# An S5 state loop on one core: VectorE works a tile off inside its bank, and output products go two tiles at a time

## The reference

```python
u = h @ w_in
bu_re, bu_im = (einsum('sbgk,gpk->sbgp', u, bb) for bb in (bb_re, bb_im))
_, _, xr, xi = lax.associative_scan(combine, (a_re, a_im, bu_re, bu_im), axis=0)
y = einsum('sbgp,gkp->bsgk', xr, c_re) - einsum('sbgp,gkp->bsgk', xi, c_im)
y = gelu(y + d_skip * u)
y = y * sigmoid(y @ w_glu)
return y @ w_o
```

## Time and profile before

| | |
|---|---|
| Time, median of 3 runs | 2179.3 us (2178.06 to 2179.93) |
| The profiled execution | 2181.11 us, of which the span from first to last instruction 2179.3 us |
| TensorE, VectorE, ScalarE, GpSimd busy | 94%, 32%, 18%, 5% of the span |
| Mean granted clock of TensorE | 0.974 of full speed |
| First product of the state loop on VectorE | 1126.11 us after the span's start |
| Last GLU block | starts at 1292.72 us |

### The profile page before, as it was taken

One profiled execution on the slowest core, in us unless ns is written; L12 is line 12 of the kernel. 1 busy time (PEld: TensorE's weight loads), 2 busy tenths in 40 slices (PEclk: granted clock), 3 DMA queues, 4 the chain that ended last, 5 costly groups with the idle time before them and its releaser, 6 DMA issues.

```text
span 2179.3 us, 29172 instructions
## 1 busy us (share of the span) xinstructions
PE 2054.0 (94%) x12304; PEld 1142.9 (52%) x12304; DVE 688.5 (32%) x1417; ACT 388.9 (18%) x821; POOL 110.9 (5%) x103
## 2 busy tenths in 40 slices
PE   7998999998999999999989985999999999999995
PEld 5577785666785766777755543233323233333322
DVE  3263212344201475344459864101101010101103
ACT  3212103212101322243320002110101010110100
POOL 0000000000000000000027640000000000000000
PEclk9999999999999999999999997999999999999998
DMA  7244465333456322433222114597988989797981
GB/s 300 82 187 156 193 241 224 116 140 143 181 232 244 135 79 87 165 151 139 116 97 107 48 75 166 232 394 299 386 329 343 377 336 383 316 404 298 391 327 58
DMA packets 41488, 472.75 MB, mean 217 GB/s; under 512 B 4645, under 2 KB 6309, under 8 KB 7881
## 3 DMA queue, kind: packets, MB, share of 16 engines
q1 hardware_dynamic: 38576, 464.39, 53.5%
q10 hardware_dynamic: 2568, 6.31, 0.8%
q0 software_dynamic: 272, 1.05, 0.1%
HBM read 470.68 MB, written 1.06 MB: 216 GB/s over the span
## 4 chain that ended last, share of the span: by engine, by line
PE 86%; DVE 7%; DMA 4%; ACT 1%; issue 1%; POOL 0%; ACTq 0%; SPq 0%; DVEq 0%; POOLq 0%
PE bank L896 19%; PE bank L545 14%; PE bank L926 10%; PE bank L848 7%; PE bank L860 3%; PE bank L712 3%; PE bank L530 3%; PE bank L537 3%; PE bank L718 3%; PE bank L558 2%; DMA arena<-in_wgu 2%; PE bank L976 2%; PE bank L967 2%; PE bank L1019 1%; PE bank L615 1%; PE bank L647 1%
## 5 line engine op out<-in xcount | busy, mean ns | idle before, releaser
L896 PE MATMUL bank<-arena 128*32 128x512 f32 x4096 | 451.8, 593 | 1.7 <-DMA arena<-in_wgu 1.4
L545 PE MATMUL bank<-arena 128*128 128x256 f32 x1408 | 321.3, 388 | 11.0 <-ACT small L1236 11.0
L545 PEld LDWEIGHTS bank<-arena 128*128 128x128 f32 x1408 | 270.7, 194 | 67.4 <-issue 17.8
L896 PEld LDWEIGHTS bank<-arena 128*32 128x32 f32 x4096 | 130.0, 110 | 309.7 <-issue 295.8
L926 PE MATMUL bank<-arena 128*32 128x512 f32 x2112 | 238.2, 595 | 0.0
L1996 DVE TENSOR_TENSOR arena<-arena,bank 128x256 f32<-128x256 f32 x64 | 26.9, 421 | 620.7 <-ACT arena L1400 584.3
L848 PE MATMUL bank<-arena 128*128 128x256 f32 x704 | 153.7, 379 | 0.1
L848 PEld LDWEIGHTS bank<-arena 128*128 128x128 f32 x704 | 133.6, 190 | 21.8 <-issue 4.1
L926 PEld LDWEIGHTS bank<-arena 128*32 128x32 f32 x2112 | 62.9, 109 | 133.3 <-issue 132.5
L1400 ACT ACTIVATE arena<-bank 128x256 f32<-128x256 f32 x64 | 24.5, 383 | 580.8 <-PE bank L896 580.8
L2206 POOL TENSOR_TENSOR arena<-arena 128x512 f32<-128x512 f32 x64 | 81.3, 1271 | 45.1 <-DVE arena L2045 42.6
(11 more groups left out here) (422 smaller groups left out, 2024.5 us busy)
## 6 DMA issues: line engine op xcount, KB each, us to landing
arena<-in_wgu SPq DMA_DIRECT2D x88, 2048.0 KB, 9.3
arena<-in_w SPq DMA_DIRECT2D x46, 2048.0 KB, 7.9
arena<-in_wdn SPq DMA_DIRECT2D x88, 1024.0 KB, 7.9
arena<-in_modw SPq DMA_DIRECT2D x24, 2048.0 KB, 9.1
arena<-in_wf SPq DMA_DIRECT2D x11, 3072.0 KB, 10.2
arena<-in_flt_deltas ACTq DMA_DIRECT2D x2, 1024.0 KB, 14.2
cst<-in_consts SPq DMA_DIRECT2D x1, 1162.0 KB, 16.7
arena<-in_x SPq DMA_DIRECT2D x1, 1024.0 KB, 5.2
```

The costliest lines, as they stand in the source:

```text
L545: ins = mm(bank[b][:, j * S:(j + 1) * S], w[:, col:col + P], hT[:, k, :], start=(k == 0), stop=(k == KT - 1))
L896: ins = mm(bank[w % 2][32 * j:32 * j + 32, :], hTe[:, k, TOK * b:TOK * b + TOK], wslot[c % RING][:, k, :], start=(k == 0), stop=(k == KT - ...
```

## The change

- VectorE (loop at L2025): the product with the cosine still goes to SBUF (`vcos`), that with the sine goes in place over the bank. The sum (formerly GpSimd's) and the difference are written into the bank too, each with one operand from `vcos` and one from the bank. The scans read the bank and come in the same step as the products. TensorE may fill the bank again after the scans (`z5_ready`), no longer after the products.
- GpSimd (L2199) keeps the two products into `cz`, which has four buffers instead of two.
- TensorE (L1029): `s5_out(o)`, in even steps, does the output products of tiles `o` and `o + 1` together, in step `o + 4`, alternating between the two tiles, which write different groups of 32 rows of the bank.
- `s5_in` blocks come a step earlier (odd steps); the GLU blocks stay. `y_tile(j)` comes in step `4j + 8` of VectorE, after the scans of tile `4j + 8` (it was after those of tile `4j + 6`).
- `w3[4]` lands at another place and is issued at `cz_ready` 12 instead of 8.

```diff
--- before.py
+++ after.py
@@ -20,7 +20,7 @@
 STATE_TILES = 32
 FR = 3
 FUSES = [len(range(r, 11, FR)) if r < FR else 0 for r in range(RING)]
-IN_HALF = {2: (1, 0), 4: (1, 1), 6: (2, 0), 8: (2, 1), 10: (3, 0), 12: (3, 1)}
+IN_HALF = {1: (1, 0), 3: (1, 1), 5: (2, 0), 7: (2, 1), 9: (3, 0), 11: (3, 1)}
 GLU_AT = {15: 0, 17: 1, 19: 2, 21: 3, 25: 4, 29: 5, 33: 6}
 TWO_PI = 6.283185307179586
 PI2_HI = 6.28125
@@ -315,8 +315,8 @@
 
         uT = view(CH * 2, 8, S)
         yT = view(CH * 2 + 2048, 8, S)
-        vpr = view(CH * 3, 2, 2, 2, S)
-        cz = view(CH * 3 + 2048, 2, 2, 2, S)
+        vcos = view(CH * 3, 2, 2, S)
+        cz = [view(at, 2, 2, S) for at in (CH * 3 + 2048, CH * 3 + 3072, W + 18432, LOW + 2048)]
         sgl = view(CH * 3, 8, S)
         zz = view(W + 2048, 2, 2, S)
         ftmp5 = view(W + 2560, 512)
@@ -332,7 +332,7 @@
         bst = [view(W + 16384, 1024), view(W + 18432, 1024)]
         cst5 = view(W, 2, 1024)
         cneg = view(W + 16384, 1024)
-        wmix = [ring[0], ring[1], ring[0], ring[1], view(LOW + 2048, CH), view(W + 5376, CH)]
+        wmix = [ring[0], ring[1], ring[0], ring[1], view(LOW + 4096, CH), view(W + 5376, CH)]
 
 
 
@@ -409,7 +409,7 @@
                 elif n < 4:
                     sp.wait_ge(sm["grp_ps"], G3 + 4)
                 else:
-                    sp.wait_ge(sm["cz_ready"], (8, 20)[n - 4])
+                    sp.wait_ge(sm["cz_ready"], (12, 20)[n - 4])
                 sp.dma_start(wmix[n], a["w3"][n]).then_inc(landeds[n % RING], 16)
                 if n == 1:
 
@@ -1026,6 +1026,23 @@
             gate_rows(3, gdiag5)
             s5_in(0, 1)
             pe.wait_ge(sm["b5t_ready"], 4)
+            def s5_out(o):
+
+                j = o // 4
+                if o == 0:
+                    pe.wait_ge(sm["c5_ready"], 1)
+                    pe.wait_ge(sm["gb_ready"], 3)
+                pe.wait_ge(sm["cz_ready"], o + 2)
+                if o % 4 == 0 and o >= 8:
+                    pe.wait_ge(sm["y_out"], j - 1)
+                for n, (which, tb, ri) in enumerate(((cst5[:, 0], 0, 0), (cneg, 1, 1), (cst5[:, 1], 0, 1), (cst5[:, 1], 1, 0))):
+                    for q in (o, o + 1):
+                        r = slice(32 * (q % 4), 32 * (q % 4) + 32)
+                        ins = mm(bank[6 + j % 2][r, 0:S], which[:, q * 32:(q + 1) * 32], cz[q % 4][:, tb, ri, :],
+                                 start=(n == 0), stop=(n == 3), skip_group_check=True)
+                        if n == 3:
+                            ins.then_inc(sm["sy_ps"], 1)
+
             for i in range(STATE_TILES + 3):
                 if i < STATE_TILES:
                     j, r = i // 4, slice(32 * (i % 4), 32 * (i % 4) + 32)
@@ -1033,24 +1050,12 @@
                         c = i // 8
                         pe.wait_ge(free[c % 2], (G3 + c) // 2 + 1)
                     if i >= 2:
-                        pe.wait_ge(sm["sv_used"], i - 1)
+                        pe.wait_ge(sm["z5_ready"], i - 1)
                     for c in range(2):
                         ins = mm(bank[4 + i % 2][:, c * S:(c + 1) * S], bT[r, c, j, :], uT[r, j, :], start=True, stop=True)
                     ins.then_inc(sm["sv_ps"], 1)
-                if i >= 3:
-                    o = i - 3
-                    j, r = o // 4, slice(32 * (o % 4), 32 * (o % 4) + 32)
-                    if o == 0:
-                        pe.wait_ge(sm["c5_ready"], 1)
-                        pe.wait_ge(sm["gb_ready"], 3)
-                    pe.wait_ge(sm["cz_ready"], o + 1)
-                    if o % 4 == 0 and o >= 8:
-                        pe.wait_ge(sm["y_out"], j - 1)
-                    for n, (which, tb, ri) in enumerate(((cst5[:, 0], 0, 0), (cneg, 1, 1), (cst5[:, 1], 0, 1),
-                                                         (cst5[:, 1], 1, 0))):
-                        ins = mm(bank[6 + j % 2][r, 0:S], which[:, o * 32:(o + 1) * 32], cz[:, o % 2, tb, ri, :],
-                                 start=(n == 0), stop=(n == 3), skip_group_check=True)
-                    ins.then_inc(sm["sy_ps"], 1)
+                if i >= 4 and i % 2 == 0:
+                    s5_out(i - 4)
                 if i in IN_HALF:
                     s5_in(*IN_HALF[i])
                 if i in GLU_AT:
@@ -2022,31 +2027,25 @@
                 v.scalar_tensor_tensor(yT[:, j, :], uT[:, j, :], ev[:, E_DSK + j:E_DSK + j + 1], bank[6 + j % 2][:, 0:S],
                                        ALU.mult, ALU.add).then_inc(sm["y_out"], 1)
 
-            for i in range(STATE_TILES + 1):
+            for i in range(STATE_TILES + 2):
                 if i < STATE_TILES:
 
                     dve.wait_ge(sm["sv_ps"], i + 1)
+                    src = bank[4 + i % 2][:, :].rearrange("p (a b) -> p a b", a=2)
+                    by_cos = vcos[:, i % 2]
+                    link(v.tensor_tensor(by_cos, src, tab[i][:, 0, :].unsqueeze(1).broadcast_to([P, 2, S]), ALU.mult))
+                    link(v.tensor_tensor(src, src, tab[i][:, 1, :].unsqueeze(1).broadcast_to([P, 2, S]), ALU.mult))
+                    link(v.tensor_tensor(src[:, 1, :], by_cos[:, 0, :], src[:, 1, :], ALU.add))
+                    link(v.tensor_tensor(src[:, 0, :], by_cos[:, 1, :], src[:, 0, :], ALU.subtract))
                     if i >= 2:
-                        dve.wait_ge(sm["w_ready"], i - 1)
-                    src = bank[4 + i % 2][:, :].rearrange("p (a b) -> p a b", a=2)
-                    p0 = vpr[:, i % 2]
-                    link(v.tensor_tensor(p0[:, 0], src, tab[i][:, 0, :].unsqueeze(1).broadcast_to([P, 2, S]), ALU.mult))
-                    v.tensor_tensor(p0[:, 1], src, tab[i][:, 1, :].unsqueeze(1).broadcast_to([P, 2, S]),
-                                    ALU.mult).then_inc(sm["sv_used"], 1)
-                    dve.wait_ge(sm["sv_used"], i + 1)
-                    link(v.tensor_tensor(wz[:, i % 2, 1, :], p0[:, 0, 1, :], p0[:, 1, 0, :], ALU.subtract))
-                if i:
-                    o = i - 1
-                    dve.wait_ge(sm["w_ready"], o + 1)
-                    if o >= 2:
-                        dve.wait_ge(sm["cz_ready"], o - 1)
-                    decay_col = mag[:, o:o + 1].broadcast_to([P, S])
-                    link(v.tensor_tensor_scan(zz[:, o % 2, 0, :], decay_col, wz[:, o % 2, 0, :], 0.0, ALU.mult, ALU.add))
-                    v.tensor_tensor_scan(zz[:, o % 2, 1, :], decay_col, wz[:, o % 2, 1, :], 0.0, ALU.mult, ALU.add)\
+                        dve.wait_ge(sm["cz_ready"], i - 1)
+                    decay_col = mag[:, i:i + 1].broadcast_to([P, S])
+                    link(v.tensor_tensor_scan(zz[:, i % 2, 0, :], decay_col, src[:, 1, :], 0.0, ALU.mult, ALU.add))
+                    v.tensor_tensor_scan(zz[:, i % 2, 1, :], decay_col, src[:, 0, :], 0.0, ALU.mult, ALU.add)\
                         .then_inc(sm["z5_ready"], 1)
-                    dve.wait_ge(sm["z5_ready"], o + 1)
-                if i >= 7 and (i - 7) % 4 == 0:
-                    y_tile((i - 7) // 4)
+                    dve.wait_ge(sm["z5_ready"], i + 1)
+                if i >= 8 and i % 4 == 0:
+                    y_tile(i // 4 - 2)
             y_tile(7)
             for c in range(4):
                 n = G3 + 4 + c
@@ -2196,26 +2195,16 @@
             pool.wait_ge(sm["xt_ps"], 16)
             link(pool.iota(iot, pattern=[[1, S]], base=0, channel_multiplier=0, allow_small_or_imprecise_dtypes=True))
             pool.memset(small[0:1, 90:91], 0.0).then_inc(sm["iota_ready"], 1)
-            for i in range(STATE_TILES + 2):
-                if i >= 2:
-                    o = i - 2
-                    pool.wait_ge(sm["z5_ready"], o + 1)
-                    if o >= 2:
-                        pool.wait_ge(sm["sy_ps"], o - 1)
-                    for n in range(2):
-                        ins = pool.tensor_tensor(cz[:, o % 2, n], zz[:, o % 2],
-                                                 tab[o][:, n, :].unsqueeze(1).broadcast_to([P, 2, S]), ALU.mult)
-                        if n == 0:
-                            link(ins)
-                    ins.then_inc(sm["cz_ready"], 1)
-                if i < STATE_TILES:
-
-                    pool.wait_ge(sm["sv_used"], i + 1)
-                    if i >= 2:
-                        pool.wait_ge(sm["z5_ready"], i - 1)
-                    p0 = vpr[:, i % 2]
-                    pool.tensor_tensor(wz[:, i % 2, 0, :], p0[:, 0, 0, :], p0[:, 1, 1, :], ALU.add)\
-                        .then_inc(sm["w_ready"], 1)
+            for o in range(STATE_TILES):
+                pool.wait_ge(sm["z5_ready"], o + 1)
+                if o >= 4:
+                    pool.wait_ge(sm["sy_ps"], o - 3)
+                for n in range(2):
+                    ins = pool.tensor_tensor(cz[o % 4][:, n], zz[:, o % 2],
+                                             tab[o][:, n, :].unsqueeze(1).broadcast_to([P, 2, S]), ALU.mult)
+                    if n == 0:
+                        link(ins)
```

(1 more changed line is left out.)

## The result

The changed kernel took 2164.1 us (2161.5 to 2165.1) against 2178.9 of the kernel before on the same chip: ratio 0.9930, 95% interval 0.9913 to 0.9947. Run again later, beside other runs of the kernel before, it came to 0.9920 (0.9907 to 0.9934). Faster, as forecast, and inside the range; 15 to 17 us instead of 21.

What follows compares the result with a forecast made beforehand. VectorE was taken to bound the S5 state loop, TensorE close behind. Shorter tiles, stalls and tail gave -29.5 us at full clock; clock falls added 8.5, leaving -21: 2158 us, range 2148 to 2172.

Steps and rivals of the forecast that it cites:

- VectorE's tile: S5 state loop: two products, addition, subtraction, two scans and gaps take 3.81 us a tile, before 4.83.
- The bounds of 0.12 for a write to a bank and of 1.09 for a scan: VectorE, state loop: upper ends for extra cost per bank write (nothing taken) and for a scan's duration (0.69 taken).
- The waits for GpSimd: State loop: VectorE instructions with two SBUF inputs wait 1.47 us a tile; one bank operand removes this. Rival, scan waits: 0.06.
- The pair: TensorE, state loop: output products of two tiles, alternating between two column groups, take 1.9 us instead of 3.7.
- the rival of no overlap: TensorE output products: a pair takes 3.6 us, giving -17, or -8 with clock falls; 2162 to 2171; chance 0.08.
- The stalls: GLU blocks 3 to 5: later y_tile makes VectorE stand 1.5 us each, 4.4 in all, plus 1.9 each for clock.
- Block 0: First GLU block: weights land after 12.8 us, 0.7 of waiting hidden; 5.61 at low clock, 0.9 reaching VectorE.
- The later start of the third load: Weight loads: w3[4] no longer leaves with the two GLU block 0 needs; those land at the old 12.8 us.
- the sum: From VectorE's first product: tiles 121.9, y_tiles 3.1, stalls 4.4, then tail; -29.5 us at full clock, +8.5 for clock falls.
- the tail: Last scans to last GLU block: 7.7 us at full clock against 9.48 before; block 6's clock fall adds 1.9.
- The bank as source and target: Rival, VectorE in-place bank instructions: two cycles an element, 1.08 us more a tile; 2181 to 2189; chance 0.08.
- The clock did not stay low: Rival, TensorE throughout the stage: clock stays low, its work doubles, +57 us; chance 0.03.

Runs made afterwards that it cites:

- e1: Changed kernel with sine product, sum and difference written to SBUF, all on VectorE, scans reading SBUF: 2187.4 us, 1.0021 of the kernel before.
- e2: Changed kernel with a pair's output products run one tile after the other instead of alternating: 2167.6 us, 0.9936 of the kernel before.
- e4: Changed kernel plus 46 unread full-width products where TensorE stands idle before and between GLU blocks, waits unchanged: 2155.5 us, 0.9868 of the kernel before.
- e3: Changed kernel with y_tile(j) one tile earlier, after the scans of tile 4j + 7: 2155.6 us, 0.9872 of the kernel before.
- e6: Changed kernel with y_tile(j) after tile 4j + 6, GLU block 6 in step 31, blocks 0 to 3 two steps later, last two weight loads later: 2146.6 us, 0.9848.
- e8: e6 plus 21 unread full-width TensorE products in steps 13, 15, 27 and 33: 2150.0 us, 0.9865 of the kernel before.

## Why the prediction was right, and where its sizes were off

**VectorE's tile.** Right to 0.02 us: 3.83 against 3.81. The bounds of 0.12 for a write to a bank and of 1.09 for a scan were far too wide. The Trainium skill ("VectorE: DVE Perf Modes", the section on the TRN2 errata) would have had a source in PSUM 62 cycles dearer; the scans are 686 from a bank and 691 from SBUF (e1), so the measurement goes against it for these instructions.

**The waits for GpSimd.** Right; e1 shows it for the sum. The rule of the Trainium skill ("SBUF — State Buffer", "Who interferes with whom") that one SBUF input does not contend agrees with the scans' 686 to 686, though only 0.28 us of the first scan lies beside GpSimd's work, and that two do with the sum's 424 to 1501. One reading of the prediction is loose: the difference that took 0.42 in the earlier trace rows had GpSimd beside it. It had started 0.05 before GpSimd did, and there GpSimd's addition took 0.96 where its median is 0.905.

**The pair.** Its time was right (1.92 against 1.9 forecast), so the rival of no overlap fell. The rival's price of 3.6 for a pair was never run: one tile after the other the pair takes 2.81 (e2). So e2 shows that alternating gives 1.4 us in the stretch with the changed VectorE; what the change would have brought with no overlap at all, -17 by the prediction, is not shown.

**The stalls.** The three behind blocks 3 to 5 were forecast at 1.5 and 1.9 for the clock, 3.4 each; they are 3.37, 3.07 and 3.94, and e4 parts them into 1.69 and the rest. This was the best hit: e3 takes away the wait for gelu and with it the whole stall, e4 only what the clock adds.

**The mis-sized terms.** Block 0 was to reach VectorE with 0.9 us; it was 3.30. The weights came 13.0 us after the last input block, as in the kernel before (the prediction says 12.8, its give 13.0). But that block ended at 1170.6 and not at 1169.4, so the wait was 2.13 and not 0.7, and block 0 took 6.48 and not 5.61. The later start of the third load did nothing for it: in e6, where the third load starts 20.1 us after the second, the second lands 12.3 us after its issue, and in the changed kernel 12.4.

At tile 4 VectorE stood 0.86 that the sum does not have: an input block there is at the low clock (5.29 at 1134.82), a fall that the prediction does not list. Together VectorE stood 14.5 us against 11.0 in the sum. And block 6 took 6.61, so the tail was 10.5 and not 9.6. With 3.5 + 0.9, less 0.4 because a y_tile put off the next tile by 0.39 and not by 0.51, the stretch of 145.6 becomes 149.6. That is the 4 us between -21 and -17. The rest, to the -15 of the medians, lies within the spread of the runs of both kernels: the second comparison gives -17.

**The other rivals.** The bank as source and target costs 8 ns, not 0.27 or 0.54 us. The clock did not stay low: 0.87 over the stretch, down from 0.94.

## What to carry to other kernels

Where one engine's instructions run longer beside another's, as VectorE's did beside GpSimd's, ask for each how many of its input tensors lie in SBUF; a result that may stay in its bank can take these waits away without any less work. After the engine that set the pace is relieved, look at each place where another engine's program waits in order: here a y_tile placed one or two tiles late, and GLU blocks in the steps where they had to wait, cost as much as the whole change gained. And idle time on TensorE has a price twice, once as waiting and once as clock, so shortening its work next to such a wait may return little (e2: 0.89 us less a pair, 16 pairs, 1.4 us in the stretch). Filling it with idle work helped here only where the clock would fall on a block that somebody waits for (e4), and cost time elsewhere (e8).

## What was not expected of the hardware

46 products that compute nothing made the stretch 9.6 us shorter (e4), by holding its granted clock at 0.98 in place of 0.87. Two pairs of output products next to each other overlap without any alternation between them (32 records in 2.82, against 1.92 for 16). The lengths of a block of eight products after a wait ran from 5.1 to 6.8 us in the two profiles of the changed kernel, against 3.72 at full clock.
